# Two filler products behind each Z of the inverse, and a re-dealt tail of row sums and normalisation, in a one-core encoder layer

## What is computed

```python
q, k, v, z, b, a, aq, ak, av, ga, gb = split(x @ w_in)
# gated DeltaNet, 8 heads of 128, chunked delta rule; per chunk and head:
lower = where(strict, (k * beta) @ k.T * decay, 0)
t_inv = triangular_solve(eye + lower, eye)        # the inverse
w, u = t_inv @ (kb * exp(gc)), t_inv @ (v * beta)
# band attention, 8 heads of 64; both branches gated, merged, projected
x = layer_norm(ALPHA * x + mix, ln1_g, ln1_b)
# mixture of experts: 64 experts, top 6 of them for each token, one shared expert
y[token] = sum over its 6 choices of weight * expert(x[token])
out = layer_norm(ALPHA * x + y + shared(x), ln2_g, ln2_b)
```

## Time and profile before

| | us |
|---|---|
| median of three runs | 1322.85 |
| lowest and highest | 1322.81, 1324.76 |
| the profiled execution | 1322.01 |
| its span in the trace | 1319.7 |

### The profile page before, as it was taken

How to read it: one execution, slowest core, us unless ns; L and a number is a source line. 1 busy time by engine, 2 the same in 40 slices (tenths; PEclk the granted TensorE clock), 3 DMA queues, 4 the chain that set the end, 5 groups by cost and what they waited for, 6 DMA issues and landing times.

```text
span 1319.7 us, 23842 instructions
## 1 busy us (share of the span) xinstructions
PE 1241.5 (94%) x8589; PEld 782.5 (59%) x8590; DVE 480.8 (36%) x945; ACT 312.1 (24%) x829; POOL 356.8 (27%) x420
## 2 busy tenths in 40 slices
PE   8999999999999989999999899988899999988996
PEld 5587778777774458888557645444454455444442
DVE  3755665556514543233246511101111211111248
ACT  3332333323322442222133011111111011111111
POOL 2545535364602341000000232322122122322101
PEclk9999999999999999999999999988899999999998
DMA  4632333233023113435834399999999999999994
GB/s 131 188 96 86 119 111 122 62 110 111 16 64 121 49 36 93 112 103 168 348 129 158 127 406 418 421 419 423 421 418 423 411 412 392 382 427 423 424 405 196
DMA packets 119599, 312.82 MB, mean 237 GB/s; under 512 B 9774, under 2 KB 79534, under 8 KB 102992
## 3 DMA queue, kind: packets, MB, share of 16 engines
q1 hardware_dynamic: 106592, 284.53, 56.5%
q0 software_dynamic: 10768, 24.72, 5.0%
q10 hardware_dynamic: 2144, 2.22, 0.6%
HBM read 289.32 MB, written 34.38 MB: 245 GB/s over the span
## 4 chain that ended last, share of the span: by engine, by line
PE 46%; DMA 10%; DVE 4%; issue 2%; ACT 0%; SPq 0%; DVEq 0%; POOL 0%; POOLq 0%
PE bank L1990 17%; PE bank L1380 11%; PE bank L1997 8%; DMA expert_gu<-in_expert_w_gate_up_dram 7%; PE bank L1386 4%; PE bank L1982 2%; DVE x_rows L2277 1%; DMA late_rows<-choice_rows 1%; PE bank L2042 1%; PE bank L2066 1%; PE bank L1408 1%; DMA choice_rows<-expert_y,row_col 1%; PE bank L1401 1%; DVE x_rows L2288 0%; DMA gathered_x<-x_rows,tok_col 0%
## 5 line engine op out<-in xcount | busy, mean ns | idle before, releaser
L1990 PE MATMUL bank<-expert_gu,gathered_xT 128*64 128x256 f32 x2016 | 254.9, 406 | 27.7 <-DMA expert_gu<-in_expert_w_gate_up_dram 17.5
L1990 PEld LDWEIGHTS bank<-expert_gu,gathered_xT 128*64 128x64 f32 x2016 | 142.9, 140 | 120.4 <-issue 24.0
L2201 DVE SCALAR_TENSOR_TENSOR hidden<-gate,slot_w,bank 128x128 f32<-128x128 f32 x64 | 22.2, 348 | 399.5 <-ACT gate L2158 388.4
L1997 PE MATMUL bank<-expert_down,hiddenT 128*64 128x512 f32 x504 | 121.8, 603 | 2.5 <-issue 2.5
L486 PE MATMUL bank<-x_high,w_head_low 128*128 128x512 f32 x224 | 93.9, 419 | 0.0
L486 PE MATMUL bank<-x_high,w_head_high 128*128 128x512 f32 x224 | 93.3, 417 | 0.0
L486 PE MATMUL bank<-x_low,w_head_high 128*128 128x512 f32 x224 | 93.2, 416 | 0.0
L2158 ACT ACTIVATE gate<-bank 128x128 f32<-128x128 f32 x64 | 17.8, 278 | 274.3 <-PE bank L1990 274.3
L1885 POOL COPY row_col<-row_idx 128x1 int32 (+1 forms) x60 | 10.9, 181 | 257.5 <-ACT expert_y L2152 197.5
L1888 POOL DMA_INDIRECT choice_rows<-expert_y,row_col x60 | 59.9, 998 | 47.4 <-POOL row_col L1885 47.4
L676 POOL TENSOR_TENSOR w_head_low<-w_head,w_head_high 128x1024 fp32r<-128x1024 f32 x28 | 66.5, 2373 | 2.2
(11 more groups left out here) (397 smaller groups left out, 2256.6 us busy)
## 6 DMA issues: line engine op xcount, KB each, us to landing
expert_gu<-in_expert_w_gate_up_dram SPq DMA_DIRECT2D x63, 2048.0 KB
expert_down<-in_expert_w_down_dram SPq DMA_DIRECT2D x63, 1024.0 KB
w_head<-in_w_in_dram SPq DMA_DIRECT2D x32, 512.0 KB, 4.2
choice_rows<-zero_rows SPq DMA_DIRECT2D x6, 2048.0 KB, 9.2
late_rows<-choice_rows SPq DMA_DIRECT2D x4, 2048.0 KB, 21.2
w_tile<-in_w_in_dram SPq DMA_DIRECT2D x14, 512.0 KB, 4.0
x_rows<-in_x_dram SPq DMA_DIRECT2D x8, 512.0 KB, 6.6
first_rows<-choice_rows SPq DMA_DIRECT2D x4, 1024.0 KB, 18.0
```

The lines of the kernel that those rows point to most:

```text
L1990: mm = nc.tensor.matmul(bank[parts[a], 0:2 * P], x[:, c, part], halves[:, a, :, :], start=(c == 0), stop=(c == KC - 1))
L1997: mm = nc.tensor.matmul(bank[parts[a], :], hidden_t[:, c * BLK:(c + 1) * BLK], dn[:, c, a * (D // 2):(a + 1) * (D // 2)], start=(c == 0), ...
```

## The change

In the inverse, `fill(20)` becomes `fill(18)`, and two filler products instead of one follow Z in each of the five levels. With 2 fewer and 5 more, 3 fewer are left behind the output's transposes: none in the first seven heads, 48 in the last.

In the tail, VectorE adds 4, 4, 4 and 3 rows instead of 5, 5, 4 and 3, so TensorE adds two in tiles 0 to 2 and three in tile 3. The first two additions of tile 0 come ahead of the last `low_y`. `SHARED_OUT` goes from 2 to 3, so tile 2 too goes by ScalarE and GpSimd and leaves in one DMA. GpSimd's addition of the offset for tile t now also waits until the first statistics of tile t + 1 are done.

```diff
@@ -569 @@ delta_phase, tensor, body
-                fill(20)
+                fill(18)
@@ -598 @@
                     mm.then_inc(zt_psum[l], 1)
-                    fill(1)
+                    fill(2)
@@ -1783 @@ experts_phase
-    SHARED_OUT = TT - 2
+    SHARED_OUT = TT - 1
@@ -1804 @@
-    BY_VECTOR = (5, 5, 4, 3)
+    BY_VECTOR = (4, 4, 4, 3)
+    EARLY_ROWS = 2
@@ -1960 @@ gpsimd
         def add_beta(t):
             pool.wait_ge(scaled, t + 1)
+            pool.wait_ge(st_done, 2 * (TT + t + 1) + 1)
             nc.gpsimd.tensor_tensor(xs[:, t, :], xs[:, t, :], b_row[:, :], ALU.add).then_inc(beta_added, 1)
@@ -2264 @@ vector
-        low_y(STEPS - 1)
-
-        def add_rows(t):
-            for k in range(BY_VECTOR[t]):
+        def add_rows(t, first, end):
+            for k in range(first, end):
@@ -2296 @@
+        add_rows(0, 0, EARLY_ROWS)
+        low_y(STEPS - 1)
+        add_rows(0, EARLY_ROWS, BY_VECTOR[0])
+        add_rows(1, 0, BY_VECTOR[1])
         dve.wait_ge(ln_in, 32)
-        add_rows(0)
-        add_rows(1)
         normalise(0)
-        add_rows(2)
+        add_rows(2, 0, BY_VECTOR[2])
         normalise(1)
-        add_rows(3)
+        add_rows(3, 0, BY_VECTOR[3])
         normalise(2)
         normalise(3)
```

## The result

| | us |
|---|---|
| the changed kernel, median of seven runs | 1314.71 (1310.45 to 1317.36) |
| the kernel before on the same chip, median of seven | 1322.81 (1318.66 to 1324.76) |
| ratio | 0.9942, 95% interval 0.9926 to 0.9958 |
| the profiled execution of the changed kernel, its span | 1316.91, 1315.3 |

What follows compares the result with a forecast made beforehand. TensorE was taken to bound the inverse, streamed weights the experts, and the tail to wait on GpSimd's offset and VectorE. 1322.01 less 7.6 (fillers) and 3.7 (tail) is 1310.7, or 1311.5 by the median; forecast 1311.0, range 1308.5 to 1315.5.

Steps and rivals of the forecast that it cites:

- (a): Inverse, turn of a head: no fillers behind the output's transposes lets L556 start 0.71 us earlier, with 0.2 of slack.
- (b): Inverse: two fewer fillers ahead of the first inverse product save 0.46 us a head, with XT done 0.2 ahead.
- (c): Inverse levels: a second filler behind Z costs 0.04 us a level, 0.16 a head, mostly covered by VectorE's subtraction.
- The rival that pays each filler in full: Inverse: each second filler delays Y by 0.23 us, leaving only the tail's gain, 1318.5 us; chance 0.07.
- the rival that the clock gives way: Inverse: denser work cuts TensorE's granted clock; at a mean of 0.93 it costs 24 us, giving 1335; chance 0.03.
- The first head: Inverse, first of eight heads: TensorE waits for XT, so fewer fillers ahead give nothing there; gain 0.55 us.
- A gain in the inverse moves all later stages earlier: Stages behind the inverse: barriers separate them, so the inverse's 7.6 us arrives whole and the experts neither add nor use it.
- a sign that the whole is wrong: Experts: their span changing by more than 1 us would show the whole prediction wrong.
- The tail up to VectorE's end: Tail: tile 3's statistics start 3.84 us earlier, at 1307.7, with TensorE ending last and VectorE idle up to 3.
- the rival that VectorE's additions stay long: Tail: a cause other than GpSimd's reads keeps additions long; tile 2's end at 1297.6, giving 1312.0 us; chance 0.05.
- Then the end is as before: Tail's end: nothing changes behind tile 3's statistics except two debits, together taken as 0.1 us.
- The debit of tile 2's output: Tail's end: tile 2's 0.5 MB output, queued on SyncE ahead of tile 3's halves, costs 0 to 0.7 us.

Runs made afterwards that it cites:

- ahead20: Changed kernel with 20 fillers ahead of the first inverse product, ten instead of 12 ahead of the output's transposes, and SHARED_OUT = 2; one execution, 1311.65 us.
- z_three: Changed kernel with three fillers behind each Z, seven instead of twelve ahead of the output's transposes, and SHARED_OUT = 2; one execution, 1318.56 us.
- fillers_only: The kernel before with only the fillers changed (18 ahead, two behind each Z), tail as before; 1314.4 us, ratio 0.9931 to the kernel before.
- after_again: The changed kernel once more, no edit; median of six 1318.2 us, ratio 0.9946 to the kernel before.
- scale2: Changed kernel with SHARED_OUT back to 2, so GpSimd adds two tiles' offsets and VectorE the third; 1311.64 us, ratio 0.9917 to the kernel before.
- drain_timed: Changed kernel plus one GpSimd drain ahead of its first offset addition in the tail, run six times; 1312.25 us, ratio 0.9917 to the kernel before.
- early_drain: Changed kernel plus one explicit GpSimd drain ahead of its first offset addition in the tail; one execution, 1309.74 us.
- scale0: Changed kernel with SHARED_OUT = 0: GpSimd adds no offset, VectorE scales and offsets all four tiles; one execution, 1310.04 us.
- drain_rows: early_drain with VectorE's rows dealt as in the kernel before (five, five, four, three, none early); one execution, 1311.3 us.
- drain_now: early_drain, but GpSimd starts each offset as soon as the normalised tile is there, as in the kernel before; one execution, 1312.43 us.

## Why the prediction was right, and where it was not

**(a), nothing behind the output's transposes: right.** Forecast -0.71 a head with 0.2 of slack to the first silu. Measured 0.43 from L648 to L556 instead of 1.14, and 0.28 of slack; ahead20 and z_three show that the slack was real and small.

**(b), two fewer ahead of the first inverse product: right.** Forecast -0.46, measured 7.82 - 7.35 = 0.47. XT was feared as the next bound and holds nobody back beyond the first head, where TensorE waits 1.2 us for it (0.8 before).

**(c), a second filler behind Z: right, and a little cheaper.** Forecast +0.16 a head. The period fell by 1.11, so +0.07 is left for it. The rival that pays each filler in full, 1318.5, is out: fillers_only gave -9.1. So is the rival that the clock gives way: it was granted 1.00 with TensorE busy 100.00 of 100.

**The first head: the row that is off.** Forecast -0.55; it takes 93.31 - 49.96 = 43.35 instead of 43.05. The timeline shows a stall for which the profile has no releaser:

```profile
66.37 0.40 PE L486 MATMUL bank<-x_high,w_head_high 128*128 128x512 f32 x1 [0.81 <-issue]
```

The same stall is 0.53 in after_again, the same kernel (43.09 for the head), and 0.25 in fillers_only (42.83). It is there in eight of the ten traces with two fillers behind Z, not in scale2 (42.39) and ahead20, and in none of the three with one filler. The change seems to bring it, but its size differs between executions of one kernel. Less the stall the head takes 42.54, 42.56 and 42.58 in the first three; 42.50 was forecast. The cause wasn't tried.

**"A gain in the inverse moves all later stages earlier": only in part.** Against the first head's transposes (49.14 and 49.96) the attention's first product (L1055, at 401.23 and 394.75) starts 352.09 us later before and 344.79 after, 7.3 less, near the forecast of 7.6. At the merge's first product (L1380, at 491.41 and 484.50) it is 7.7 less. At the first expert product it is 700.78 against 704.36, so only 3.6 are left. 1.5 us go between the first products of L1380 and those of L1386 (149.4 before, 150.9 after, with L1380's products at 0.63 instead of 0.40 in the first 4 us), and 2.6 at the entry of the experts: from L1984's first transposes to L2044's it takes 750.48 - 740.64 = 9.84, before 753.25 - 745.98 = 7.27. The windows there (start and end, and then as in the first fence), of the changed kernel and then of drain_timed, which has the same code up to the tail:

```profile
740.00:744.00 4.00, 2.49 (x12) 1.98 (x14) 1.38 (x2) 0.00 (x0) 1.77 (x4) 0.60 0.40 145
744.00:748.00 4.00, 4.00 (x24) 2.42 (x22) 0.00 (x0) 0.00 (x0) 0.00 (x0) 0.55 0.01 5
```

```profile
740.00:744.00 4.00, 2.96 (x27) 2.28 (x28) 0.92 (x2) 0.00 (x0) 0.77 (x3) 1.00 0.21 68
744.00:748.00 4.00, 4.00 (x37) 2.64 (x34) 1.66 (x3) 0.38 (x2) 0.88 (x2) 1.00 0.44 132
```

The granted clock, as a mean of each window, is 0.60 and 0.55 in one, so at its lower level, 1.2 GHz, for some 7 of these 8 us, and at the full 2.4 GHz in the other. In the changed kernel it fell behind a wait of 1.91 us for the gathered rows; the kernel before had waited 1.89 at that place and kept the full clock. Where neither stretch appears the gain does arrive: in early_drain, scale0, drain_timed, drain_rows and drain_now the first expert product comes 697.07 to 697.30 behind the first transposes, 7.1 to 7.3 less than before. The experts then take 517.3 in the changed kernel from their first to their last product, before 519.4. That is a change of 2.1, and more than 1 was named as a sign that the whole is wrong. The sign was too narrow: over all traces this span lies between 517.0 and 520.0, whichever code ran ahead of it. Whether the stream of weights makes up for a late start wasn't tried. Over the traces, the last expert product starts between 1262.7 and 1268.0 in the ten with two fillers behind Z, and between 1272.3 and 1275.0 in the three with one. The two means differ by 7.2, about the forecast of 7.6; the changed kernel's own trace got 4.9. Why one kernel meets the low clock there and another doesn't stays open.

**The tail up to VectorE's end: right.** Forecast -3.84 from the product on tile 2's first_rows to tile 3's statistics, measured -4.06. TensorE ends last, VectorE is idle for 2.43 ahead of it (up to 3 forecast), and no addition is longer than 1.42. So the rival that VectorE's additions stay long is out. One reading of the kernel before was too simple: the working took TensorE's wait of 2.13 and its products at half clock for what held tile 3 back. There VectorE went into tile 3's statistics without idle time, just as TensorE ended (1311.47 and 1311.53), so both paths ended together, and fillers_only shows that without the half clock nothing moves. The number came out because the change shortens both paths, TensorE's by 4.06 and VectorE's by that and 2.43 more.

**"Then the end is as before": the step that failed.** The working priced the third offset on GpSimd by when VectorE could go on, and took 0.1 for both debits. It didn't ask what closes the block. In the kernel before, GpSimd's drain ended 9.0 behind its last addition and 3.0 ahead of SyncE. The change gives GpSimd a third offset. Its last addition then ends 1.25 ahead of VectorE's last write (1304.75 and 1306.00), where it had ended 9.8 ahead (1306.18 and 1315.96). So the drain turned from 3 us early to 5.0 us late. After tile 3's statistics the kernel before needed 8.2 us, the changed one 13.7, drain_timed 8.9. The row was in the trace of before: a drain of 11.45 us on POOLq at the last line. Of an engine that gets one more piece of work near the end, the price runs to the end of its drain, not of its instruction.

**The debit of tile 2's output: at its upper bound.** With the drain out of the way the rest behind VectorE's last write is 4.4 to 4.5, before 3.7: 0.7, where 0 to 0.7 had been the bounds and 0.1 was taken. The tail's true term is then 46.8 - 43.4 = 3.4 or so, against 3.7.

So the sum of the two terms, -11.3, is what the change gives once the drain is paid early: 0.9917 of 1323 is -11.0 (-13.2 to -8.7). The changed kernel as it is gives -7.7. The closeness of -11.0 to -11.3 is finer than these measurements: the two halves by themselves gave -9.1 and, with the early drain, -4.5.

**What stays open.** That the 9 us belong to the phase and not to an instruction is shown by early_drain and scale0. What they are isn't. This phase is the one in which GpSimd issues indirect DMAs, 108 of them in the trace of before; the drains of the three earlier phases took 0.33, 0.60 and 2.52 us. A run without those DMAs wasn't made, so that link is only argued.

## What to carry to other kernels

Price the last work of every engine to the end of its drain: read the drain rows at each block's end, in the kernel before, and compare each with the last landing that SyncE waits for. Where an engine owes a long drain, let it drain where it waits anyway; here one instruction gave 5.8 us in one kernel (the intervals apart) and 3.8 in another (overlapping a little). Where fillers are moved, look at what the place that loses them was covering: here the three behind the output's transposes could go with a gain, while each of the two or five taken from ahead of them added about 0.2 us to the head's period.

## What the runs showed of the hardware that had not been expected

- GpSimd's first drain in the last phase takes 8.98 to 9.31 us in five kernels in which no addition of the tail ran ahead of it, and ends 9.0 us behind the last addition where one did. The second drain in the same phase takes none of it (1.5 us, which ends with the addition in front of it).
- Stretches at the lower clock, of some 4 to 7 us, appear in some kernels and not in others whose code is the same at that place, and cost 1.5 us at the merge and 2.6 at the entry of the experts. In the tail of the kernel before such a stretch cost nothing, and the same tail in fillers_only ran without it behind the same wait.
- TensorE stalled for 0.25 to 0.81 us in the middle of a row of fillers, in the first head of eight of fourteen traces, with nothing that the profile shows as its releaser.
